# Weight splits in two halves of the contraction, with a signal for each, in a decoder-step kernel on one core

## What is computed

```python
for l in range(DEPTH):
    hp = rms_norm(xp, norm_mix[l])
    ...
    xp = xp + op
    mk, mv = memory_kv(mem_prompt, norm_mem[l], w_ca_kv[l])
    xp = xp + cross_attn(rms_norm(xp, norm_ca[l]), mk, mv, w_ca_q[l], w_ca_o[l])
    xp = xp + swiglu(rms_norm(xp, norm_ffn[l]), w_ffn_in[l], w_ffn_out[l])
    ...
y_prompt = rms_norm(xp, norm_final)
```

## Time and profile before

| | |
|---|---|
| median of 3 runs | 3247.64 us (3246.01 to 3248.03) |
| the profiled execution | 3247.53 us, its span 3245.8 us |
| TensorE busy (PE) | 3030.2 us, 93% |
| weight loads (PEld) | 2871.3 us, 88%, beside the products |
| VectorE busy | 1426.1 us, 44% |
| POOL busy | 866.1 us, 27%: 246 x L438 and 246 x L441 |
| ScalarE busy | 651.3 us, 20% |
| granted TensorE clock, mean | 0.980 of full |
| HBM read, written | 184.34 MB, 13.10 MB: 61 GB/s over the span |

### The profile page before, as it was taken

One profiled execution on the slowest core, in us unless ns is written; L12 is line 12 of the kernel. 1 busy time (PEld: TensorE's weight loads), 2 busy tenths in 40 slices (PEclk: granted clock), 3 DMA queues, 4 the chain that ended last, 5 costly groups with the idle time before them and its releaser, 6 DMA issues. The chain is left out here.

```text
span 3245.8 us, 53467 instructions
## 1 busy us (share of the span) xinstructions
PE 3030.2 (93%) x20003; PEld 2871.3 (88%) x20003; DVE 1426.1 (44%) x2798; ACT 651.3 (20%) x1565; POOL 866.1 (27%) x497
## 2 busy tenths in 40 slices
PE   6999899889999999999789998998999999999996
PEld 5888798779999999999777776988889999999996
DVE  5344642235444444444843235522254444444446
ACT  3222522222100000000313235211232000000002
POOL 2212133232333333333211111233223333333331
PEclk9999899999999999999899999999999999999998
DMA  3001123321111111111121121133311111111111
GB/s 119 27 32 32 34 86 119 118 103 45 46 45 45 45 45 50 47 45 46 34 93 72 40 72 53 45 137 120 132 39 41 51 45 45 45 45 45 50 47 59
DMA packets 52491, 198.28 MB, mean 61 GB/s; under 512 B 6960, under 2 KB 14000, under 8 KB 49080
## 3 DMA queue, kind: packets, MB, share of 16 engines
q1 hardware_dynamic: 36912, 130.51, 12.3%
q10 hardware_dynamic: 15504, 66.71, 5.6%
HBM read 184.34 MB, written 13.10 MB: 61 GB/s over the span
## 5 line engine op out<-in xcount | busy, mean ns | idle before, releaser
L475 PE MATMUL linear<-h_hi,w_hi 128*128 128x344 f32 x3312 | 1075.5, 325 | 56.8 <-POOL w_lo L441 14.3
L475 PE MATMUL linear<-h_lo,w_hi 128*128 128x344 f32 x3312 | 1067.9, 322 | 0.0
L475 PE MATMUL linear<-h_hi,w_lo 128*128 128x344 f32 x3312 | 1066.8, 322 | 0.0
L438 POOL TENSOR_SCALAR w_hi<-w_raw 128x1024 fp32r<-128x1024 f32 x246 | 265.0, 1077 | 2307.3 <-PE linear L475 2297.7
L475 PEld LDWEIGHTS linear<-h_hi,w_hi 128*128 128x128 f32 x3312 | 631.0, 191 | 67.8 <-issue 46.2
L475 PEld LDWEIGHTS linear<-h_lo,w_hi 128*128 128x128 f32 x3312 | 630.9, 190 | 0.7 <-issue 0.2
L475 PEld LDWEIGHTS linear<-h_hi,w_lo 128*128 128x128 f32 x3312 | 631.0, 191 | 0.0
L441 POOL TENSOR_TENSOR w_lo<-w_raw,w_hi 128x1024 fp32r<-128x1024 f32 x246 | 600.8, 2442 | 20.5
L1320 DVE TENSOR_TENSOR x<-linear,x 128x344 f32<-128x344 f32 x528 | 272.3, 516 | 212.3 <-PE linear L475 212.0
L475 PE MATMUL linear<-hid_hi,w_hi 128*128 128x344 f32 x1056 | 340.3, 322 | 7.9 <-DVE x L1320 7.9
L475 PE MATMUL linear<-hid_hi,w_lo 128*128 128x344 f32 x1056 | 340.2, 322 | 0.0
(11 more groups left out here) (191 smaller groups left out, 3221.8 us busy)
## 6 DMA issues: line engine op xcount, KB each, us to landing
w_raw<-in_w SPq DMA_DIRECT2D x246, 512.0 KB, 3.5
kv_slotc<-in_mem_cache_k ACTq DMA_DIRECT2D x8, 2048.0 KB, 8.5
kv_slotc<-in_mem_cache_v ACTq DMA_DIRECT2D x8, 2048.0 KB, 10.1
kv_slot<-in_dil_k ACTq DMA_DIRECT2D x4, 1536.0 KB, 7.5
kv_slot<-in_dil_v ACTq DMA_DIRECT2D x4, 1536.0 KB, 6.8
out_y<-answer ACTq DMA_DIRECT2D x6, 688.0 KB, 3.5
x<-in_x ACTq DMA_DIRECT2D x2, 1376.0 KB, 10.4
out_dil_k_out<-k ACTq DMA_DIRECT2D x4, 516.0 KB, 2.7
```

Source lines behind the costliest of these rows:

```text
L438: pool.tensor_scalar(w_hi[:, s, :], w_raw[:, s, :], 1.0, 0.0, ALU.mult, ALU.add).then_inc(pool_hi, 1)
L475: mm = pe.matmul(out, w[:, slot, cols], a, start=(k == 0 and j == 0), stop=(k == n - 1 and j == 2))
```

## The change

POOL makes four passes of 512 columns a unit where it made two of 1024: `w_hi` of the first half of the columns, `w_hi` of the second, then `w_lo` of the first half, which raises a new signal `half_split`, and `w_lo` of the second, which raises `unit_split`. TensorE starts a unit on `half_split`. In the unit's first accumulation alone it waits for `unit_split` before the chunk with which the second half begins: the fifth of eight, ahead of the 13th product, or in `down` the second of two, ahead of the fourth. SyncE's wait is as before.

```diff
         if units:
-            events |= {"unit_split": units, "unit_started": units}
+            events |= {"half_split": units, "unit_split": units, "unit_started": units}
...
-                    pool.tensor_scalar(w_hi[:, s, :], w_raw[:, s, :], 1.0, 0.0, ALU.mult, ALU.add).then_inc(pool_hi, 1)
-
-                    pool.wait_ge(pool_hi, 2 * i + (s + 1))
-                    pool.tensor_tensor(w_lo[:, s, :], w_raw[:, s, :], w_hi[:, s, :].bitcast(F32), ALU.subtract
-                                       ).then_inc(sem["unit_split"], 1)
+                    for half in range(2):
+                        c = slice(D // 2 * half, D // 2 * half + D // 2)
+                        pool.tensor_scalar(w_hi[:, s, c], w_raw[:, s, c], 1.0, 0.0, ALU.mult, ALU.add).then_inc(pool_hi, 1)
+
+                    for half, event in enumerate(("half_split", "unit_split")):
+                        c = slice(D // 2 * half, D // 2 * half + D // 2)
+                        pool.wait_ge(pool_hi, 4 * i + (2 * s + half + 1))
+                        pool.tensor_tensor(w_lo[:, s, c], w_raw[:, s, c], w_hi[:, s, c].bitcast(F32), ALU.subtract
+                                           ).then_inc(sem[event], 1)
...
-            def passes(out, slot, terms, unit_first=False, ready=None):
+            def passes(out, slot, terms, unit_first=False, ready=None, second_half=None):
 
                 n = len(terms)
                 for k, (cols, hi, lo) in enumerate(terms):
+                    if second_half is not None and k == n // 2:
+
+                        pe.wait_ge(sem["unit_split"], second_half)
...
-                pe.wait_ge(sem["unit_split"], at("unit_split", phase, turn, u + 1))
+                pe.wait_ge(sem["half_split"], at("half_split", phase, turn, u + 1))
...
-                           unit_first=(t == 0), ready=ready and (lambda k: ready(t, k)))
+                           unit_first=(t == 0), ready=ready and (lambda k: ready(t, k)),
+                           second_half=at("unit_split", phase, turn, u + 1) if t == 0 else None)
...
-                    pe.wait_ge(sem["unit_split"], at("unit_split", ph, i, u + 1))
+                    pe.wait_ge(sem["half_split"], at("half_split", ph, i, u + 1))
...
-                                    for k in range(2)], unit_first=(t == 0 and n == 0))
+                                    for k in range(2)], unit_first=(t == 0 and n == 0),
+                                   second_half=at("unit_split", ph, i, u + 1) if t == 0 and n == 0 else None)
```

## The result

The changed kernel takes **3217.85 us** (median of 4 runs, 3216.33 to 3218.73) against 3247.64 us before: a ratio of 0.9909, 95% interval 0.9892 to 0.9926, or 29.8 us less. The forecast was 3233 us with a range from 3225 to 3241 us. The profiled execution took 3216.33 us, its span 3214.5 us.

The account below looks back on a forecast made before the run. TensorE, busy 93% of the span, was taken as the bound, so only its waits for POOL's w_lo could pay. 15.1 us won in the heads less 1.0 us for added waits gave 14.1 us off: 3233 us, range 3225 to 3241.

Parts of the forecast that it names:

- At the start ... I count nothing: Kernel start: the first product could go earlier, but x's second tile lands only at 20.91 us; nothing counted, at most 0.9 us.
- the low bound of 3224 us: Cheap halves rival, chance 0.13: no fixed part per pass, 0.04 us gap, 0.08 us restart, the start's 0.9 us won.
- The 15.1 us of the heads: Cross-attention heads: TensorE's three waits for w_lo shrink by 1.89 us in a head, times 8.
- first wait: First of a head's three TensorE waits for w_lo: start at 2176.17 instead of 2177.04 us, 0.87 us won.
- second wait: Second of a head's three TensorE waits for w_lo: start at 2191.67 instead of 2192.57 us, 0.90 us won.
- third wait, its own part: Head's third wait: 1.02 us won including the second's 0.90; POOL's pace goes only from 4.29 to 4.16 us a unit.
- With the 0.08 us gap between passes: POOL's split of a unit: 0.08 us between passes, so the first half is ready after 2.62 us instead of 3.5 us.
- The restart after a satisfied wait: POOL turning to the next unit at a head's third wait: taken as 0.20 us, between 0.08 and 0.27 us.
- 246 x 4 ns = 1.0 us lost: TensorE's one added wait per unit, nearly all satisfied when reached, costs about 4 ns each.
- the two stretches: Feed-forward steps: projections, a wait per 24 products, 157.6 ns; down products, a wait every 6, 158.3 ns; about 4 ns a wait.
- the slower rival: Waits inside an accumulation stop TensorE's weight loads, 0.19 us each, 46.7 us lost, 3279 us; decides from 61 ns; chance 0.05.
- from about 27 us to about 12 us: Sign in the profile after: fall of TensorE's waits in the heads for w_lo or its half.

Follow-up runs that it names:

- interleaved: The changed kernel with POOL's order w_hi first half, w_lo first half, w_hi second half, w_lo second half; 3207.69 us.
- quarters: The interleaved kernel with four w_hi and four w_lo passes of 256 columns a unit, signals after the second and fourth w_lo; 3228.65 us.
- experiment 6: The kernel before with half passes and early start only in the 198 units outside the cross-attention phases, whole passes in their 48; 3238.75 us.
- experiment 4: The kernel before with only an added, always satisfied unit_split wait inside each unit's first accumulation; 3246.44 us against 3246.42.
- the late start: The changed kernel's half passes, but TensorE starts a unit only on unit_split, with no wait inside an accumulation; 3238.81 us.

## Why the prediction was wrong

**The step that failed outright is "At the start ... I count nothing", and with it the sum's silence on VectorE.** It took 20.91 us, ScalarE's start on x's second tile, as given; it came at 18.37 us. I costed POOL's passes only by when they release TensorE. They also hold VectorE. The feed-forward shows it row by row; every third `hid_lo` meets a `w_lo` pass, the other two take 0.52 us. Before, changed, interleaved, and quarters, each a POOL row and the VectorE row that meets it:

```profile
1202.45 2.54 POOL L441 TENSOR_TENSOR w_lo<-w_raw,w_hi 128x1024 fp32r<-128x1024 f32 x1
1203.29 2.08 DVE L1312 TENSOR_TENSOR hid_lo<-hid,hid_hi 128x344 fp32r<-128x344 f32 x1 [0.56 <-ACT hid_hi L784]
```

```profile
824.20 1.29 POOL L445 TENSOR_TENSOR w_lo<-w_raw,w_hi 128x512 fp32r<-128x512 f32 x1
824.31 1.55 DVE L1321 TENSOR_TENSOR hid_lo<-hid,hid_hi 128x344 fp32r<-128x344 f32 x1 [0.56 <-ACT hid_hi L793]
```

```profile
1186.66 1.43 POOL L443 TENSOR_TENSOR w_lo<-w_raw,w_hi 128x512 fp32r<-128x512 f32 x1
1187.50 0.97 DVE L1319 TENSOR_TENSOR hid_lo<-hid,hid_hi 128x344 fp32r<-128x344 f32 x1 [0.56 <-ACT hid_hi L791]
```

```profile
1193.69 0.88 POOL L443 TENSOR_TENSOR w_lo<-w_raw,w_hi 128x256 fp32r<-128x256 f32 x1
1194.52 0.52 DVE L1320 TENSOR_TENSOR hid_lo<-hid,hid_hi 128x344 fp32r<-128x344 f32 x1 [0.56 <-ACT hid_hi L792]
```

The first three end 0.37 or 0.38 us after the pass does, wherever in the pass they start and whatever its length. In the changed kernel that is the end of the first of two `w_lo` passes, though the second starts without a gap. In the quarters `hid_lo` meets only the pass's last 0.05 us, and no hold is seen; that is a matter of where it falls. The mean of the 132 follows: (0.52 + 0.52 + 2.08) / 3 = 1.04 us before, 0.86 us with 1.55 and 0.67 us with 0.97 in the place of 2.08. The Trainium skill (SBUF — State Buffer, Who interferes with whom) states that a VectorE instruction with two SBUF inputs contends with a GpSimd instruction that reads SBUF, for a port pair that the two engines share and that is an exclusive lock. The traces agree: VectorE ends 0.38 us after the pass, and `rs<-ps_turned` at 11.86 us, with one operand in PSUM, is not held.

In the feed-forward nothing came of it, as VectorE has slack there (0.0 us). Where TensorE waits for VectorE it counts. In the changed kernel 2.7 us are won by the product of 34 us, before the clocks of the two traces part; 0.6 of them are x's first tile, which leaves 2.1 (in experiment 6 it is 2.3 less 0.1). Two waits into layer 1 give 2.3 us, and the end 0.9: 5.3 us. At the end the held `hid_lo` (2.04 us before, 0.97 after) lets TensorE go on after 2.75 us instead of 3.66; the other 1.2 of the table's 2.1 us go with a shorter stretch at half clock behind it. Experiment 6 gives 7.5 us for all of this, such a stretch at its end included. So of the 9.9 us outside the heads some 5 us go with VectorE's holds; most of the rest goes with the clock, and no run separates it further. The rows for this were in the trace of before: 2.22 us for an instruction that takes 0.56 elsewhere. Nor did any rival hold it, so that the low bound of 3224 us, with all costs at their ends, was still 6 us too high.

**The 15.1 us of the heads came to 21.0 us.** Starts of units after unit 0 of the head, in us: 15.71, 19.83, 24.11 before, 14.67, 17.74, 21.48 after.

| term | predicted | measured |
|---|---|---|
| first wait | 0.87 | 1.04 |
| second wait | 0.90 | 1.05 |
| third wait, its own part | 0.12 | 0.54 |
| a head | 1.89 | 2.63 |
| a unit on POOL, two in a row | 4.16 | 3.75 |

The mis-sized steps are the gap and the restart. "With the 0.08 us gap between passes" took the gap of a dependent pass for every gap: from the first `w_hi` to the first `w_lo` it is 1.17 us, not 1.36, since none of the three waits for a pass that is still running. The restart after a satisfied wait, taken at 0.20 us, is 0.04. Together with 0.06 us at the two `w_lo` this is the 0.41 us between 4.16 and 3.75. The half pass itself was nearly right: 0.62 and 1.29 us instead of 0.60 and 1.26, a fixed part of 2 x 0.62 - 1.05 = 0.19 and 2 x 1.29 - 2.37 = 0.21 us; the quarters in a head, at 0.41 and 0.74 us, give 0.20 and 0.19. The Trainium skill's figure (GPSIMD Engine Reference, Performance versus the Vector engine), from which I had estimated 0.24 us, was closer than my 0.15. Its forecast of 3237 us was farther off all the same, since what decided was the overlap of passes.

**"246 x 4 ns = 1.0 us lost"** was nothing: experiment 4, and 726.21 us twice. The 4 ns were not what the two stretches gave, either: the down products have one wait more in eight steps (1/6 - 1/24), so 0.7 ns a step would have been 5.5 ns a wait, 1.4 us in all. With it falls the slower rival.

In the traces 31.2 us were won where the sum had 14.1. Of the 17.1 us between them the heads are 6, the waits that cost nothing 1, and the stages outside the heads 10, a term of which the sum had none.

What held: the place and number of the waits, the second wait as good as gone (2169.28 to 2169.60 us is 0.32, with a step of 0.12), the third still there, no gap before the 13th product, the feed-forward unchanged, no new wait at the attention. Of what was to show it, "from about 27 us to about 12 us" came out as 18.0 - 13.2 = 4.8 us in the view, which names only the third wait; from start to start the three are 31 us before and 10 us after. And POOL's passes on the page are 0.67 and 1.35 us on average, over the bound that I had set at 1.34. That bound was no test of the fixed part: VectorE holds POOL as well, and in the heads, where it does not, they are 0.62 and 1.29.

## What to carry to other kernels

Before costing a change of a GpSimd pass, look for VectorE instructions of one shape with two durations, and see what ran on GpSimd in the longer ones; in every such pair here the rest of the pass it meets sets the hold. Split such a pass so that its dependent parts alternate and the consumer starts on the first. Stop where the fixed part of the passes (0.2 us each here) costs the producer's pace more than the earlier start wins. With consumers of 2.9 us in a row, the heads won 26 us at 3.99 us a unit and 8.5 at 4.8; in all, halves won 30 to 40 us here, quarters 19.

## What the runs showed of the hardware

GpSimd passes that wait for nothing unfinished overlap by 0.04 us, a pass that waits for the one before follows after 0.08 us, and behind a satisfied wait on another engine's signal the next starts 0.04 us after the last has ended.

Stretches of half clock (1.2 GHz) on TensorE come and go between these kernels, and move the time by 1 to 4 us. Windows of before (columns: us, PE, PEld, DVE, ACT, POOL busy, granted clock, DMA share, GB/s), after, and interleaved:

```profile
3191.00:3195.90 4.90, 2.37 (x15) 2.09 (x14) 3.71 (x5) 0.49 (x1) 3.43 (x2) 1.00 0.01 2
3195.90:3202.70 6.80, 5.98 (x21) 5.99 (x22) 4.81 (x11) 2.40 (x5) 0.00 (x0) 0.50 0.00 0
```

```profile
1635.00:1639.00 4.00, 4.00 (x16) 4.00 (x17) 0.00 (x0) 0.00 (x0) 3.15 (x4) 0.59 0.82 276
...
3167.50:3170.90 3.40, 3.40 (x14) 3.40 (x13) 3.07 (x7) 1.51 (x4) 0.00 (x0) 0.50 0.03 5
```

```profile
1634.40:1638.00 3.60, 3.60 (x23) 3.60 (x24) 0.00 (x0) 0.00 (x0) 2.83 (x4) 1.00 0.81 260
...
3155.00:3160.00 5.00, 3.03 (x20) 2.74 (x18) 3.56 (x7) 0.49 (x1) 4.30 (x4) 1.00 0.01 2
```

At the end TensorE stood 3.66 us before and 2.75 us after, and then ran at half clock for 6.8 and 3.4 us; in the interleaved kernel, which stood there too, it kept 2.4 GHz. The same at att1: beside the rows above, the granted clock was 0.56 from 1653 to 1657 us before, and 1.00 from 1648 to 1652 us with the late start. What makes the difference stays open, so the 3.4 us at att1 and the 2 us at the end are no gain of the order of passes that another kernel can count on.
